# A two-block transformer kernel: ada pieces placed among x's turns, ScalarE writes that scale and shift, padded rotary queries, square sums in two passes

## The chip, the core and the metric

The kernel runs on one core of a Trainium2 chip. Five engines work from queues of their own and meet at semaphores: TensorE (PE, its weight loads listed apart as PEld), VectorE (DVE), ScalarE (ACT), GpSimd (POOL) and SyncE (SP), which here only issues DMAs. The metric is the time of one execution in microseconds. "Time" below is the device time of a run; "span" is the stretch that the profiler shows of one execution.

## What is computed

Two layers' worth of blocks on 512 tokens of width 2048, with 256 context tokens in the first. All is float32.

```python
# first block (cut)
sh_x, sc_x, gt_x = split(silu(c) @ w_ada + b_ada, 3)         # the same for the context with c_ctx
h_x = rms_norm(x, norm_g) * (1 + sc_x) + sh_x
h_c = rms_norm(ctx, norm_g) * (1 + sc_c) + sh_c
px, pc = split_cols(h_x @ w_in), split_cols(h_c @ w_in)
oa, ob, oc, od = mixer_a(px[0:4], ...), mixer_b(...), mixer_c(...), mixer_d(...)   # four attentions
x = x + gt_x * (concat([oa, ob, oc, od]) @ w_out)
# mixer d: q and k have 128 plain and 64 rotary columns per head;
#   s = q_nope @ k_nope.T + q_rope @ k_rope.T, softmax, @ v, times silu(gate)
# second block: an even and an odd layer
h = rms_norm(x, g) @ w_in;  q = rms_norm(heads(h_q), q_gain);  k = rms_norm(heads(h_k), k_gain)
#   heads are 64 wide, so each 128-row tile holds two heads; pooling, top-k attention, window attention
x = x + (silu(gate) * o) @ w_out
```

## The kernel before

**Data and products.** Activations lie transposed: a tile is 128 features by the tokens. A product with large weights is made of three TensorE passes over numbers of the type fp32r: each operand is split into `hi` (the fp32 value rounded on a write by ScalarE) and `lo` (what is left), and `w_hi*h_hi`, `w_hi*h_lo`, `w_lo*h_hi` are summed in PSUM. Weights come as groups of 1 MB (`raw`, two buffers). ScalarE's `hi(G, half)` rounds half a group (L862), GpSimd's `lo(G, half)` subtracts (L1180), and each waits for TensorE to leave that half's buffer. A group of the late part is 16 tiles of features by three passes of 128x512, which is 48 matmuls.

**The opening** (`start` on each engine). SP loads six tiles of x and context, then the pieces of w_ada (`ada`, four pieces of 1 MB to a chunk, eight chunks, a ring of four buffers) and the weight blocks. ScalarE sums squares and takes the root of each tile (L783, L786), VectorE scales (L1314), TensorE turns the tile in 16 transposes into the four PSUM banks of `acc`, and `x_out` empties them into `X6`: banks 0 and 1 by VectorE, 2 and 3 by ScalarE. Then TensorE takes the four pieces of chunk 0 (`piece`), ScalarE copies the row (`ada_row`, L797), TensorE folds it (`fold`), VectorE adds the bias (`columns`, L1328 and L1333). Each chunk gives four tiles' scale (chunks 0 to 3) or shift (chunks 4 to 7). A small table of distances (L1299, L1301) is made first of all.

**Eight blocks** follow: for the gates of mixers a and b, products run as soon as four tiles' scale is there, without the shift. `scaled(c)` on VectorE multiplies (L1343), ScalarE rounds (L803), VectorE subtracts (L1352). TensorE works through block n in two halves; after each of the four column tiles j of half 0 it takes a piece of chunk n+1, and after j = 1 of half 1 the fold. From block 5 on the full h is made for later groups: GpSimd adds `hi` and `lo` back together once the block that read them is done (`full_sum`, L1164), VectorE scales and shifts the context tile (L1359), adds the shift to the latent tile (L1361), ScalarE rounds 768 columns (L809), VectorE subtracts (L1369). After the last block VectorE empties the banks (`gates_out`, L1379); the first group of mixer a's keys waits for all of it (`raw_out` 8) and then, tile by tile, for `h_full`.

**Mixer d.** Its last ten groups, of kinds kn and vn, multiply plain fp32 data with no split (`acc<-raw,ckv_t`). VectorE's `norm` takes a reciprocal (L1417) and two scalings (L1427, L1436). In `attend`, `scores(n)` makes for each of 16 units a 512 and a 256 wide product with 128 rows (`k_latent`), and into the same place one with 64 rows (`k_rope,q_rope`): rows 0 to 63 or 64 to 127 of the tile by the head's parity.

**The late part** (`late`) is a list of groups written out in `plan`. Of kind norm and kvn there are 27. For them ScalarE squares the product (`post`, L1108), TensorE sums the squares of 64 rows with one fp32 matmul by a matrix of ones (`first`, for the group before, after tile k = 3 of the next group; k = 5 after a group of kind wout), ScalarE takes the root and VectorE the reciprocal and the scaling (`after`, L1782, L1797). `hooks` put attention work between the tiles of the groups of kind silu: units dsa(0), dsa(1) after tiles k = 3 and 7 of the first, units swa(0), swa(1) after k = 7 and 15.

## Time and profile before

| | us |
|---|---|
| median of 3 runs | 2930.26 |
| lowest and highest | 2928.46 and 2931.2 |
| the profiled execution | 2931.68 |
| its span | 2929.8 |
| TensorE busy | 2823.2 (96%) |
| VectorE / ScalarE / GpSimd busy | 1116.1 / 959.2 / 1077.7 |

The profiled execution takes 1.88 us more than its span; a change of the span is taken as a change of the time. A row of the timeline has the start in us, the duration, the engine, the line, the operation, output and inputs, the count, and in brackets the idle time before it with what ended it. Matmuls overlap, so their pace is read from the distance of the starts.

### The profile page before, as it was taken

The numbers are of one execution on the slowest core, as the hardware profiler recorded it, in microseconds if no ns is written. First come the engines' busy times: TensorE is split into PE (matmuls) and PEld (weight loads), VectorE is DVE, ScalarE is ACT, GpSimd is POOL, SyncE is SP. The second block draws the span as 40 slices with busy tenths as digits, with TensorE's granted clock in tenths as the row PEclk, the third lists the DMA queues.
The fourth block names the chain that finished last, engine by engine and source line by source line (L and its number), as shares of the span: only waits on it lengthen the run. The fifth ranks groups of instructions, "written<-read, shape, count | busy, mean of one in ns | idle before, by whom it ended". The sixth has DMA issues, their size and how long they took to land.

```text
span 2929.8 us, 34587 instructions
## 1 busy us (share of the span) xinstructions
PE 2823.2 (96%) x14062; PEld 2176.6 (74%) x14062; DVE 1116.1 (38%) x1848; ACT 959.2 (33%) x1479; POOL 1077.7 (37%) x529
## 2 busy tenths in 40 slices
PE   5979999989999998899999999999999999999999
PEld 3557788878778874478887677766787877777787
DVE  4164323142322143322212468744223455566411
ACT  4222332242233221332222312365322223666411
POOL 1253213213321330135543343444455343545443
PEclk9989999999999999999999999999999999999999
DMA  8844412213575231413433233322443333322442
GB/s 324 298 154 124 136 58 72 72 26 101 172 180 115 62 83 43 129 36 112 122 90 87 72 101 87 101 71 74 148 122 104 100 87 94 87 76 78 138 123 83
DMA packets 456605, 318.28 MB, mean 109 GB/s; under 512 B 32352, under 2 KB 404960, under 8 KB 455680
## 3 DMA queue, kind: packets, MB, share of 16 engines
q1 hardware_dynamic: 424400, 280.09, 32.9%
q10 hardware_dynamic: 32048, 35.98, 4.8%
q8 instruction: 112, 1.84, 0.3%
q14 instruction: 45, 0.37, 0.0%
HBM read 299.14 MB, written 28.95 MB: 112 GB/s over the span
## 4 chain that ended last, share of the span: by engine, by line
PE 92%; DVE 3%; DMA 2%; ACT 1%; issue 1%; POOL 1%; SPq 0%; ACTq 0%; DVEq 0%; POOLq 0%
PE acc L1863 77%; PE aux L1863 8%; PE ssq L1866 3%; PE ssq L1863 3%; DMA raw<-in_w_in 1%; PE aux L1866 1%; POOL w_lo L1180 1%; DVE rstd L1417 1%; DVE x_t L1361 0%; PE acc L1866 0%; DVE x_t L1359 0%; DMA dist_mask_sb<-in_dist_mask 0%; DVE h_lo L1369 0%; ACT w_hi L862 0%; DVE p L1489 0%
## 5 line engine op out<-in xcount | busy, mean ns | idle before, releaser
L1180 POOL TENSOR_TENSOR w_lo<-raw,w_hi 128x1024 fp32r<-128x1024 f32 x362 | 868.7, 2400 | 1698.8 <-ACT w_hi L862 1698.6
L1863 PE MATMUL acc<-h_hi,w_hi 128*128 128x512 f32 (+1 forms) x3232 | 1214.0, 393 | 33.6 <-DVE gate_raw L1379 19.7
L1863 PE MATMUL acc<-h_hi,w_lo 128*128 128x512 f32 (+1 forms) x3232 | 1172.2, 380 | 0.0
L1863 PE MATMUL acc<-h_lo,w_hi 128*128 128x512 f32 (+1 forms) x2464 | 872.7, 376 | 0.0
L862 ACT ACTIVATE w_hi<-raw 128x1024 fp32r<-128x1024 f32 x362 | 383.0, 1059 | 1171.0 <-PE acc L1863 1077.0
L1863 PEld LDWEIGHTS acc<-h_hi,w_hi 128*128 128x128 f32 x3232 | 585.0, 188 | 206.9 <-issue 77.2
L1863 PEld LDWEIGHTS acc<-h_hi,w_lo 128*128 128x128 f32 x3232 | 583.6, 188 | 119.4
L1863 PEld LDWEIGHTS acc<-h_lo,w_hi 128*128 128x128 f32 x2464 | 440.9, 189 | 91.1 <-issue 10.6
L1863 PE MATMUL acc<-out_t_lo,w_hi 128*128 128x512 f32 x768 | 299.0, 389 | 0.0
L1417 DVE RECIPROCAL rstd<-rstd 128x512 f32<-128x512 f32 (+1 forms) x29 | 118.0, 4070 | 352.8 <-ACT rstd L906 352.7
L1863 PEld LDWEIGHTS acc<-out_t_lo,w_hi 128*128 128x128 f32 x768 | 144.3, 188 | 29.0
L1863 PE MATMUL acc<-k_t,q_t 64*128 64x256 f32 (+6 forms) x592 | 130.3, 434 | 2.8 <-DVE v_nat L1407 1.3
L1782 DVE RECIPROCAL rstd<-rstd 128x512 f32<-128x512 f32 x27 | 90.5, 3352 | 73.5 <-ACT rstd L1083 73.5
L1866 PE MATMUL ssq<-ident_sb,p 128*128 128x128 f32 x744 | 107.7, 281 | 6.3 <-ACT p L960 5.3
L1866 PEld LDWEIGHTS ssq<-ident_sb,p 128*128 128x128 f32 x744 | 82.3, 142 | 33.3 <-issue 23.3
L1863 PEld LDWEIGHTS acc<-k_t,q_t 64*128 64x128 f32 (+1 forms) x592 | 67.4, 194 | 39.0 <-issue 33.9
L995 ACT ACTIVATE p_t<-ssq 128x768 f32<-128x768 f32 (+2 forms) x64 | 49.3, 771 | 110.0 <-PE ssq L1866 110.0
L1736 DVE TENSOR_TENSOR scaled<-acc,rstd_n 128x512 f32<-128x512 f32 x62 | 42.9, 692 | 108.7 <-PE acc L1863 108.6
L1679 DVE COPY p<-cols_sb 128x4 f32<-128x4 f32 x32 | 66.2, 2068 | 0.0
L1069 ACT ACTIVATE p<-p,u_neg_max 128x257 f32<-128x257 f32 (+1 forms) x128 | 60.3, 473 | 9.8 <-DVE u_neg_max L1686 9.6
L1797 DVE SCALAR_TENSOR_TENSOR q_t<-scaled,cols_sb,rstd 128x512 f32<-128x512 f32 x24 | 62.8, 2617 | 0.9
L1754 DVE SCALAR_TENSOR_TENSOR h_lo<-x_t,cols_sb,h_hi 128x512 fp32r<-128x512 f32 x32 | 41.4, 1294 | 54.0 <-DMA x_t_dram<-x_t 54.0
(235 smaller groups left out, 2337.2 us busy)
## 6 DMA issues: line engine op xcount, KB each, us to landing
raw<-in_w_in SPq DMA_DIRECT2D x52, 1024.0 KB, 5.9
raw<-in_even_w_in SPq DMA_DIRECT2D x41, 1024.0 KB, 5.6
raw<-in_odd_w_in SPq DMA_DIRECT2D x36, 1024.0 KB, 5.6
ada_ring<-in_w_ada SPq DMA_DIRECT2D x32, 1024.0 KB, 5.5
gate_ring<-in_w_ada SPq DMA_DIRECT2D x16, 1024.0 KB, 7.0
raw<-in_w_out SPq DMA_DIRECT2D x16, 1024.0 KB, 5.9
raw<-in_even_w_out SPq DMA_DIRECT2D x16, 1024.0 KB, 5.9
raw<-in_odd_w_out SPq DMA_DIRECT2D x16, 1024.0 KB, 6.5
```

Source lines behind the costliest of these rows:

```text
L862: A.activation(WH[half][:], RAW[G.rs][:, half * HALF * P:(half + 1) * HALF * P], ACT.Copy).then_inc(S["hi_done"], 1)
L995: A.activation(PTS[u % 2][:, 0:nk], SSQ[:, 0:nk], ACT.Copy).then_inc(S["pt_ready"], 1)
L1069: e = A.activation(p, p, ACT.Exp, bias=LNG[:, c:c + 1], scale=-1.0, accum_out=LSM[:, c:c + 1])
L1180: G_.tensor_tensor(WL[half][:], RAW[G.rs][:, half * HALF * P:(half + 1) * HALF * P], WH[half][:].bitcast(F32), ALU.subtract).then_inc(S["l ...
L1417: Vv.reciprocal(RS, RS).then_inc(S["rs_done"], 1)
L1679: Vv.tensor_copy(p[:, :, :, 256], sink.unsqueeze(2).to_broadcast([P, 2, 2]))
L1736: e = Vv.tensor_tensor(Y[G.y][:], a, RSN[:], ALU.mult)
L1754: Vv.scalar_tensor_tensor(out=ktile(H2L, G.j, SEQ), in0=ktile(X, G.j, SEQ), scalar=norm_gain(G), in1=ktile(H2H, G.j, SEQ).bitcast(F32), op ...
L1782: Vv.reciprocal(RS[:], RS[:]).then_inc(S["rs_made"], 1)
L1797: e = Vv.scalar_tensor_tensor(out=out_of(G), in0=y[:], scalar=gain(G), in1=RS[:], op0=ALU.mult, op1=ALU.mult)
L1863: return M.matmul(out_, lhsT, rhs, start=start, stop=stop, skip_group_check=True)
L1866: return M.transpose(out_, in_, IDENT[rows, rows])
```

## The change

- **Order of loads.** SP loads all six tiles, then ada pieces 0 and 1, the first weight block, pieces 2 and 3, and only then the distance table's inputs. Its products on TensorE come after fold 0, its sums on VectorE after `scaled(0)`.
- **Turns.** TensorE turns tiles 0 to 3, piece 0, tile 4, pieces 1 and 2, tile 5, piece 3. ScalarE empties a turned tile two steps later than it squares (`x_out(t - 2)`), and of odd tiles only bank 3; VectorE takes the other three.
- **Scale and shift.** `scaled_hi`, `full_hi` apply scale or shift as they round; VectorE's one `scalar_tensor_tensor` (L1381, L1399 of the changed kernel) gives `lo`. VectorE, not GpSimd, adds `hi` and `lo` back. The context is made apart, one chunk to each of blocks 4 to 7 (`context`). `full_hi` stands ahead of the next weights' `hi`, and ScalarE empties the last banks.
- **Padded queries.** GpSimd clears 128x2048 numbers (`QRP`, on h1_lo's last tiles), VectorE copies each head's 64 rows into them, and `scores` multiplies 128 rows.
- **Square sums.** ScalarE writes the square twice, as fp32 and rounded; GpSimd subtracts; TensorE sums `hi` and `lo` in two fp32r passes. Between two groups of which the first is a norm and the second is not silu, the sum comes after k = 10, and ScalarE's and VectorE's `after` behind `hi(G.next, 0)` and `take(G)`; elsewhere after k = 6 (norm or wout before) or 3.

```diff
@@ SP start @@
-                for t in range(2):
+                for t in range(6):
                     sp.dma_start(ktile(XNAT, t, D), x_rows(t)).then_inc(S[f"xi{t}"], 16)
...
-                ada(0)
+                ada(0, (0, 1))
                 weights(blocks[0])
+                ada(0, (2, 3))
@@ ScalarE start @@
-                    if t:
-                        x_out(t - 1)
+                    if t >= 2:
+                        x_out(t - 2)
+                blocks = item["blocks"]
+                x_out(4)
+                hi(blocks[0], 0)
                 x_out(5)
...
+                    act.wait_ge(S["scales"], c + 1)
                     for k in range(4 * c, 4 * c + 4):
-                        act.wait_ge(S["hs_ready"], k + 1)
-                        A.activation(lat(H1H, k), lat(X6, k), ACT.Copy).then_inc(S["hs_hi"], 1)
+                        A.activation(lat(H1H, k), lat(X6, k), ACT.Identity,
+                                     scale=ADA[:, 2 * (KT + k):2 * (KT + k) + 1]).then_inc(S["hs_hi"], 1)
...
+                def context(c):
+                    act.wait_ge(S["ada_cols"], 5 + c)
+                    for k in range(4 * c, 4 * c + 4):
+                        A.activation(ctxt(X6, k), ctxt(X6, k), ACT.Identity, bias=ADA[:, 2 * k + 1:2 * k + 2],
+                                     scale=ADA[:, 2 * (KT + k) + 1:2 * (KT + k) + 2]).then_inc(S["hc_ready"], 1)
+                    act.wait_ge(S["hc_ready"], 4 * c + 4)
+                    for k in range(4 * c, 4 * c + 4):
+                        e = A.activation(ctxt(H1H, k), ctxt(X6, k), ACT.Copy)
+                    e.then_inc(S["hc_hi"], 1)
@@ VectorE start @@
                 def full(c):
+                    dve.wait_ge(S["half_done"], 2 * item["blocks"][4 + c].g + 2)
                     for k in range(4 * c, 4 * c + 4):
+                        Vv.tensor_tensor(lat(X6, k), lat(H1L, k).bitcast(F32), lat(H1H, k).bitcast(F32),
+                                         ALU.add).then_inc(S["h_sum"], 1)
@@ VectorE, mixer d @@
+                for h in range(4):
+                    rows = slice(64 * (h % 2), 64 * (h % 2) + 64)
+                    Vv.tensor_copy(ktile(QRP, h, SEQ)[rows, :], ktile(QR, h // 2, SEQ)[rows, :])\
+                      .then_inc(S["pad_done"], 1)
...
+                if G.kind == "kn" and G.j == 1:
+                    pad_queries()
@@ TensorE, scores @@
-                            e = mm(dst, ktile(QR, h // 2, SEQ)[rows, qt * P:(qt + 1) * P],
-                                   ktile(KR, h // 2, TOK)[rows, key:key + w], False, True)
+                            e = mm(dst, QRP[:, h * SEQ + qt * P:h * SEQ + (qt + 1) * P],
+                                   ktile(KR, h // 2, TOK)[:, key:key + w], False, True)
@@ late: ScalarE, GpSimd, TensorE @@
-                        A.activation(scratch(G)[0][:], Y[G.y][:], ACT.Square).then_inc(S["sq_made"], 1)
+                        A.activation(scratch(G)[0][:], Y[G.y][:], ACT.Square)
+                        A.activation(squares(G)[0][:], Y[G.y][:], ACT.Square).then_inc(S["sq_made"], 1)
...
+                        pool.wait_ge(S["sq_made"], G.norm + 1)
+                        need(pool, "sq_summed", G.norm)
+                        G_.tensor_tensor(low[:], scratch(G)[0][:], high[:].bitcast(F32), ALU.subtract)\
+                          .then_inc(S["sq_low"], 1)
...
-                        mm(SSQ[:, 0:SEQ], ONES64[:], scratch(G)[0][:], True, True).then_inc(S["sq_summed"], 1)
+                        mm(SSQ[:, 0:SEQ], ONESR[:], high[:], True, False)
+                        mm(SSQ[:, 0:SEQ], ONESR[:], low[:], False, True).then_inc(S["sq_summed"], 1)
...
-                    at_first = 5 if prev is not None and prev.kind == "wout" else 3
+                    at_first = 10 if behind(G, prev) else 3
+                    if prev is not None and prev.kind in ("wout", "norm") and not behind(G, prev):
+                        at_first = 6
```

TensorE's queue at the start of the program, up to the first block's first product, before. `ada_ring` holds the pieces, `rel_bias_sb` belongs to the distance table:

```order
L1863 MATMUL ssq<-onehot_sb,rel_bias_sb 32x512
L1863 MATMUL ssq<-onehot_sb,rel_bias_sb 32x128
L1866 MATMUL acc<-ident_sb,x_natural 128x128 x96
L1863 MATMUL aux<-ada_ring,cond_silu 32x512 x16
L1863 MATMUL ssq<-fold_sb,ada_rows 128x2 x4
L1863 MATMUL acc<-h_hi,w_hi_60 128x512
```

And now:

```order
L1917 MATMUL acc<-ident_sb,x_natural 128x128 x64
L1914 MATMUL aux<-ada_ring,cond_silu 32x512 x4
L1917 MATMUL acc<-ident_sb,x_natural 128x128 x16
L1914 MATMUL aux<-ada_ring,cond_silu 32x512 x8
L1917 MATMUL acc<-ident_sb,x_natural 128x128 x16
L1914 MATMUL aux<-ada_ring,cond_silu 32x512 x4
L1914 MATMUL ssq<-fold_sb,ada_rows 128x2 x4
L1914 MATMUL ssq<-onehot_sb,rel_bias_sb 32x512
L1914 MATMUL ssq<-onehot_sb,rel_bias_sb 32x128
L1914 MATMUL acc<-h_hi,w_hi_60 128x512
```

The table's two products moved behind the fold, and three of the four pieces moved among the turns of tiles 4 and 5.

ScalarE's queue from block 6's `hi(G.next, 0)` to the first rows of mixer a's groups, before (`w_hi` is `hi`, `ada_rows` is `ada_row`, `h_hi` is `full_hi`):

```order
L862 ACTIVATE w_hi_60<-raw_59 128x1024
L797 ACTIVATE ada_rows<-aux 128x512
L862 ACTIVATE w_hi_61<-raw_59 128x1024
L809 ACTIVATE h_hi<-x_t_116 128x768 x4
L862 ACTIVATE w_hi_60<-raw_58 128x1024
L862 ACTIVATE w_hi_61<-raw_58 128x1024
L809 ACTIVATE h_hi<-x_t_116 128x768 x8
```

The same stretch of block 6 now:

```order
L898 ACTIVATE w_hi_60<-raw_59 128x1024
L833 ACTIVATE x_t_117<-x_t_117,ada_sb 128x256 x4
L837 ACTIVATE h_hi<-x_t_117 128x256 x4
L811 ACTIVATE ada_rows<-aux 128x512
L898 ACTIVATE w_hi_61<-raw_59 128x1024
L826 ACTIVATE h_hi<-x_t_117,ada_sb 128x512 x4
L898 ACTIVATE w_hi_60<-raw_58 128x1024
```

Eight small writes for the context now stand between the weights' `hi` and the row that the fold waits for, and the rounding of h stands ahead of the next weights.

GpSimd's queue in two neighbouring late groups of kind norm, before and then now:

```order
L1180 TENSOR_TENSOR w_lo_62<-raw_59,w_hi_60 128x1024
L1180 TENSOR_TENSOR w_lo_63<-raw_59,w_hi_61 128x1024
L1180 TENSOR_TENSOR w_lo_62<-raw_58,w_hi_60 128x1024
L1180 TENSOR_TENSOR w_lo_63<-raw_58,w_hi_61 128x1024
L1180 TENSOR_TENSOR w_lo_62<-raw_59,w_hi_60 128x1024
```

```order
L1210 TENSOR_TENSOR w_lo_62<-raw_59,w_hi_60 128x1024
L1210 TENSOR_TENSOR w_lo_63<-raw_59,w_hi_61 128x1024
L1304 TENSOR_TENSOR squares_lo<-squares_173,squares_hi 128x512
L1210 TENSOR_TENSOR w_lo_62<-raw_58,w_hi_60 128x1024
L1210 TENSOR_TENSOR w_lo_63<-raw_58,w_hi_61 128x1024
L1304 TENSOR_TENSOR squares_lo<-squares_173,squares_hi 128x512
```

Each norm group gained one subtraction behind both halves of the next weights.

## Rows read from the trace of the kernel before

**Rows 1.** Timeline, all engines, 0 to 60 us: the opening's end.
```profile
39.11 3.64 PE L1863 MATMUL aux<-ada_ring,cond_silu 128*32 128x512 f32 x32
...
42.82 0.60 ACT L797 ACTIVATE ada_rows<-aux 128x512 f32<-128x512 f32 x1 [2.95 <-PE aux L1863]
...
43.47 1.05 PE L1863 MATMUL ssq<-fold_sb,ada_rows 128*128 128x2 f32 x8 [0.72 <-ACT ada_rows L797]
...
51.89 0.76 PE L1863 MATMUL acc<-h_hi,w_hi 128*128 128x512 f32 x1 [7.37 <-DVE h_lo L1352]
```
**Rows 2.** Stretches: PE, PEld, DVE, ACT, POOL busy; clock, DMA share, GB/s.
```profile
32.00:34.00 2.00, 0.04 (x1) 0.07 (x2) 2.00 (x3) 2.00 (x3) 0.00 (x0) 1.00 0.76 278
...
50.00:52.00 2.00, 0.11 (x1) 0.14 (x1) 1.94 (x4) 1.18 (x3) 0.00 (x0) 0.50 1.06 389
```
**Rows 3.** What PE's matmuls waited for, whole span: total us, times, longest.
```profile
PE acc L1863 <- DVE gate_raw L1379: 19.7, 1, 19.7
PE aux L1863 <- DVE k_rope L1436: 17.4, 2, 9.3
...
PE acc L1863 <- DVE h_lo L1352: 9.1, 4, 7.4
...
PE ssq L1863 <- POOL sq_sum L1274: 2.6, 2, 1.3
```
**Rows 4.** Timelines of ScalarE and TensorE in block 5.
```profile
150.59 0.60 ACT L797 ACTIVATE ada_rows<-aux 128x512 f32<-128x512 f32 x1
...
153.35 0.95 PE L1863 MATMUL ssq<-fold_sb,ada_rows 128*128 128x2 f32 x8
```
**Rows 5.** Timelines between block 7 and the first keys, and behind.
```profile
190.83 2.02 DVE L1369 TENSOR_TENSOR h_lo<-x_t,h_hi 128x768 fp32r<-128x768 f32 x1
...
201.99 2.48 DVE L1379 COPY gate_raw<-acc 128x512 f32<-128x512 f32 x4
...
204.52 1.01 PE L1863 MATMUL acc<-h_hi,w_hi 128*128 128x512 f32 x2 [19.67 <-DVE gate_raw L1379]
...
209.70 0.51 PE L1863 MATMUL acc<-h_hi,w_lo 128*128 128x512 f32 x2
210.05 0.51 PE L1863 MATMUL acc<-h_hi,w_hi 128*128 128x512 f32 x2
```
**Rows 6.** Timeline of VectorE, mixer d's second kn group.
```profile
1138.11 4.95 DVE L1417 RECIPROCAL rstd<-rstd 128x768 f32<-128x768 f32 x1 [1.03 <-ACT rstd L906]
```
**Rows 7.** Timelines of TensorE: fp32 products of one shape; a unit of attention d.
```profile
1185.73 8.34 PE L1863 MATMUL acc<-raw,ckv_t 128*128 128x512 f32 x19
...
1245.71 1.02 PE L1863 MATMUL acc<-k_latent,q_t 128*128 128x512 f32 x2
...
1248.97 0.33 PE L1866 MATMUL aux<-ident_sb,o_nat 128*128 128x128 f32 x1
```
**Rows 8.** Timelines of ScalarE and GpSimd around the last late norm group.
```profile
2471.84 1.06 ACT L862 ACTIVATE w_hi<-raw 128x1024 fp32r<-128x1024 f32 x1 [2.14 <-PE acc L1863]
2477.28 1.06 ACT L862 ACTIVATE w_hi<-raw 128x1024 fp32r<-128x1024 f32 x1 [4.38 <-PE acc L1863]
2478.25 0.61 ACT L1108 ACTIVATE squares<-scaled 128x512 f32<-128x512 f32 x1
...
2483.63 1.06 ACT L862 ACTIVATE w_hi<-raw 128x1024 fp32r<-128x1024 f32 x1 [2.14 <-PE acc L1863]
...
2478.42 2.37 POOL L1180 TENSOR_TENSOR w_lo<-raw,w_hi 128x1024 fp32r<-128x1024 f32 x1 [3.04 <-ACT w_hi L862]
...
2494.22 1.04 POOL L1249 TENSOR_TENSOR p<-p,u_inv 128x512 f32<-128x512 f32 x1
```
**Rows 9.** Timelines behind the last norms: TensorE at dsa(1), swa(1); VectorE before swa(1).
```profile
1897.10 0.47 PE L1863 MATMUL acc<-select_mask,ident_r 128*128 128x256 f32 x2 [2.02 <-DVE q_t L1797]
...
2489.99 1.13 PE L1863 MATMUL acc<-k_t,q_t 64*128 64x256 f32 x8
...
2489.22 0.08 DVE L1686 DVE_READ_ACCUMULATOR2_ANT u_neg_max<- 128x1 f32 x1
```

217 lines of the change are left out of this document (126 added, 91 removed).

## The prediction

> **What bounds the kernel now.** TensorE is busy for 2823.2 of 2929.8 us, so a change is worth what it takes from TensorE's idle time or from the passes it makes. I read the waits of its matmuls first [rows 3]. The largest single wait is 19.7 us, for VectorE's emptying of the banks after the eighth block; then come two waits of 17.4 together in mixer d, for VectorE's scaling, and four of 9.1 for `lo` of h, of which one is 7.4. The change touches the first and the third, and it may lengthen the second. Next I read the opening: the first block's first product starts at 51.89, after 7.37 us of nothing [rows 1]. The loads are no reason for that: the DMA engines run dry within the stretch 32 to 34 (share 0.76, then nothing is asked for until ring buffers come free), so all tiles, chunk 0 and the first weights lie there by about 33.5 [rows 2]. Last I read the pace of passes: a half group of 24 late matmuls takes 2477.28 - 2471.84 = 5.44 us, 0.227 each, and the half with a square sum 2483.63 - 2477.28 = 6.35, so one sum costs 0.91 [rows 8].
>
> **The opening.** Before, all four pieces stood behind the last turn: 3.64 from 39.11, then the row copy (0.60), the fold (1.05), and multiply, round, subtract [rows 1]. Now three of four pieces are placed among the turns, and ScalarE no longer waits for a turn before the next square. The loads then set the pace: a piece is 1.05 MB, 2.7 us at 389 GB/s [rows 2], so if piece 3 is there at 33.5, piece 2 was at 30.8. It takes 0.9 (a quarter of 3.64), the last turn about 2, and ends near 33.8; piece 3 goes to 34.8; row copy and fold take 0.65 and 1.05, to 36.6; two small additions 0.5. The distance table's products come there too, but beside ScalarE's writes. Two writes of 0.6 by ScalarE and one subtraction of about 0.8 lead to 39.3. One step can slip, so I take 40.4: **11.5 us less**, between 8 (a turn and its copies late by 3) and 13 (no slip).
> Before, the clock stood at 0.50, which is 1.2 GHz, when the first block began, after 7.37 idle, while at 32 to 34, with TensorE idle as well but for a shorter time, it was 1.00, which is 2.4 GHz [rows 1, 2]. The new order leaves no gap like the 7.37, so I let the first products run at full clock. A start at half clock cost the first keys 2.4 us (below); here, with shorter passes of pieces among them, I take 1.9, between 0 and 2.4.
>
> **The blocks.** VectorE's multiply goes, so the wait at the start of blocks 1 to 3 goes too: 9.1 - 7.4 = 1.7 less [rows 3]. Against it, on ScalarE eight context writes stand ahead of `ada_row` in blocks 4 to 6. Their price isn't in the trace; 1024 columns take 1.06 and 512 take 0.60 [rows 1, 8], so 256 cost at most 0.37 and in a row about 0.27; with one wait for themselves eight are 2.6 (2.2 to 3.0). The row's copy ended at 151.19 and the fold began at 153.35 [rows 4], a slack of 2.1. So each fold comes 0.5 late, queued behind it on TensorE the rest of the block: three times 0.5, **1.5 more** (0 to 3). The sum of the blocks is 1.7 + 1.9 - 1.5 = **2.1 less**.
>
> **Behind the last block.** The 19.67 us [rows 5] were VectorE making h for the tiles with everything behind `full_sum`, and only then four copies of 2.48 together. Now three copies by ScalarE run inside the block and the fourth, 0.60, right behind it: with semaphores 0.85. That is **18.8 less**. What is late next? Weights: `hi(G.next, 1)` then takes 1.06 and GpSimd's `lo` 2.4, to 4.4 us after the block's end, and TensorE wants them after eight tiles of three pairs at 0.35 [rows 5], 8.4 us after it starts. h: the last four tiles need four sums, four writes and four subtractions. VectorE's h_lo took 2.02 while GpSimd ran [rows 5]; even so they end about 9.5 us after the block, and tile 12 is wanted after 0.85 + 12.6. Both are covered. The clock: the first keys ran their first eight pairs in 209.70 - 204.52 = 5.18 us and not in 8 x 0.35 [rows 5]: **2.4 less**.
>
> **Mixer d.** One call of `scores` takes 1248.97 - 1245.71 = 3.26 us [rows 7]. Products of one shape take 0.43 each, a load of weights with each of them (19 in 8.34) [rows 7]. By that pace 4 of 512 and 4 of 256 columns are 1.71 + 0.85 = 2.56. The 0.70 more lies where 128 rows and 64 rows alternate. Padding makes all of them one shape with the same columns. Two ends: nothing (rows 64 of the k tile still cost) and 0.70; I take 0.65, as the fp32 products with fresh weights each time are the same case: 16 x 0.65 = **10.4 less**.
> The Trainium skill, "TensorE: Matmul & The Clock Gate", Part 2, "Step-by-step: what each phase is for", says that weight loads are pulled ahead of running matmuls where row groups don't conflict or the background buffer takes them, and that row count doesn't matter for the time; by it the padding is free and the gain the full 0.70. The same page's table in "Why this matters for your kernels" speaks against padding: products with few rows could run side by side in separate row groups. No run here shows that, and beside a 128-row product there is no free group.
> The padding costs VectorE four copies of 64x512. Nearest are the four copies of 128x512 that took 2.48 out of PSUM [rows 5]; out of SBUF they can be up to half as long: 1.3 to 2.5. They stand ahead of the reciprocal at 1138.11, which had waited 1.03 [rows 6], and TensorE waits 9.3 for what follows it [rows 3]: 0.3 to 1.5 more; I take **0.7 more**. GpSimd's clearing is hidden in its idle time.
>
> **Late sums.** Two fp32r passes are 2 x 0.227 = 0.45 in place of 0.91 [rows 8]: 0.42 to 0.46 less. 27 x 0.42 = **11.3 less**. GpSimd's low square must be there: counted from a group's end, ScalarE rounds weights (1.2) and squares twice (to 2.4), GpSimd subtracts weights (to 3.6) and then the low square, for which the nearest row has 1.04 and I allow 1.3 [rows 8], to 4.9. TensorE asks for it after 11 tiles, 11 x 0.68 = 7.5: slack 2.6. On the two places where silu follows it asks after 7 tiles, 4.8, so 0.1 late; and there everything behind is late by the new place: 3 tiles are 2.05. dsa(1) had already waited 2.02 for the scaled queries [rows 9], so it waits **2.1 more**; for swa(1) VectorE was done at 2489.30 and TensorE came at 2489.99 [rows 9], so of 2.4 late **1.7** show. After the two closing wout groups the sum is asked for one tile, 0.68, later, and the two waits of 2.6 [rows 3] shrink by **1.3**. Together 11.3 - 2.1 - 1.7 + 1.3 = **8.8 less**.
>
> The Trainium skill, "SBUF — State Buffer", "Who interferes with whom", speaks against the new work on GpSimd: GpSimd and VectorE operations with two SBUF inputs hold one port pair alone, and the other blocks. The row of 2.02 [rows 5] agrees. VectorE's longest work in a norm group is not waited for by TensorE, so the sum is as above by either.
>
> **Sum.** 11.5 + 2.1 + 18.8 + 2.4 + 10.4 - 0.7 + 8.8 = 53.3. Against the profiled execution's 2931.68 that is 2878.4; the median is 1.4 lower, so I say **2877**. With each term at its ends it is 2868 to 2888.
>
> **The rivals.**
> *Part of the new order waits elsewhere* (0.16). SP's queue holds every load in one line, and ScalarE has the block's longest list; if chunk 2's pieces, which stand behind the distance table, or `full_hi` come late, TensorE waits in blocks. For it: ScalarE's eight new writes. Against it: the DMA engines move 389 GB/s when asked [rows 2], which is a block's 5.2 MB in 13.5 us, and a block has 48 passes of 0.227, four pieces of 0.9 and a fold, 15.5 at least. Price: 1.5 to 3 us in each of six blocks, so 2886 to 2895.
> *The row change isn't what costs 0.70* (0.07): an accumulating pair on one bank would cost the same with 128 rows. Against it: the 19 products accumulate too. Price 10.4: 2887.
> *More than forecast* (0.12): the opening starts at 38.5, the dsa and swa delays are taken up by later hooks, folds aren't late: 2877 - 2 - 3.8 - 1.5, so 2866 to 2871.
> *Slower than before* (0.02): GpSimd's low square misses its place in each norm group. Each group then waits for it, and the wait comes 25 times. It decides from 2.6 us of delay; the whole gain of 53 is gone when each is 2.1 beyond that, 4.7 later than I work out, which would need two more weight subtractions ahead of it. Price: 2877 + 25 x 2.5, so 2940.
> That the change doesn't do what it says: the blocks' order would still give the 18.8; it is inside the first rival.
>
> **Chances.** Forecast 0.62, and 0.01 for anything near no change. The range 2865 to 2894 holds all but the slow case and the far part of the first rival. A measurement here tells about 0.2%, 6 us, from no change: faster 0.97, same 0.01, slower 0.02.
>
> **What would show it.** First block product near 40, clock 1.00; folds in blocks 4 to 6 with ScalarE's row as releaser, 0.5 each; the 19.67 replaced by under 1 us; `scores` in 2.6; the half group with a sum in 5.9; a wait of 4 at dsa(1). Wrong would be a wait of more than 1 us in blocks 1 to 3, VectorE's or ScalarE's h as releaser in the first keys, or the low square as TensorE's releaser in norm groups.

## The result, and the profile after

The changed kernel takes **2883.11 us** (median of 4 runs, 2882.11 to 2885.66) where the kernel before, in the same session, took 2930.02 (4 runs, 2928.46 to 2931.2): a ratio of 0.9838, 95% interval 0.9826 to 0.985. The prediction said 2877 and a range of 2865 to 2894: faster was right, the time is 6.1 us above the point and inside the range. The profiled execution has a span of 2880.3 against 2929.8, 49.5 us less, where the terms summed to 53.3. Of the 6.1 us, 3.7 are the terms' (the profiled execution took 2882.11, forecast 2878.4); the rest is that the profiled execution of before lay 1.4 above the median that the forecast used, and the one of the changed kernel lies 1.0 below its own.

The waits of TensorE's matmuls come first, as in [rows 3] (what waited and for what: total us, times, longest):

```profile
PE aux L1914 <- DVE k_rope L1472: 18.1, 2, 10.0
...
PE ssq L1914 <- ACT ada_rows L811: 3.9, 4, 1.1
PE aux L1914 <- DMA ada_ring<-in_w_ada: 3.1, 1, 3.1
PE acc L1914 <- ACT gate_raw L859: 2.2, 1, 2.2
```

The 19.7 for the gate's banks has become 2.2, and the four for `lo` of h (9.1) are down to one of 1.4. New are 3.1 for a load of an ada piece, and three of the four waits in the line of `ada_rows`, near 1.1 each.

A total of waits doesn't say where time went, because a wait is not all that a late engine costs. So I took the same instruction in both traces and subtracted its starts; what the difference grows by between two places is what the stretch between them gained.

| the same instruction | before | after | earlier by | the stretch gained | forecast |
|---|---|---|---|---|---|
| first block product | 51.89 | 40.57 | 11.3 | 11.3 | 11.5 |
| last fold, in the seventh block | 170.14 | 163.73 | 6.4 | -4.9 | +2.1 |
| first keys | 204.52 | 180.76 | 23.8 | 17.4 | 18.8 |
| first square sum behind them | 227.01 | 201.01 | 26.0 | 2.2 | 2.4 |
| first scores of mixer d | 1194.99 | 1167.31 | 27.7 | 1.7 | -0.7 |
| total sum of the first residual stream | 1472.11 | 1432.60 | 39.5 | 11.8 | 10.4 |
| last transposes | 2925.65 | 2876.13 | 49.5 | 10.0 | 8.8 |

One row is badly wrong: the blocks were to gain 2.1 us and lost 4.9. The other six are within 2.4 of the forecast, three above it and three below.

**The blocks.** TensorE, then ScalarE, in the fifth block (n = 4) of the changed kernel:

```profile
124.34 1.05 PE L1914 MATMUL ssq<-fold_sb,ada_rows 128*128 128x2 f32 x8 [1.05 <-ACT ada_rows L811]
```
```profile
119.41 1.06 ACT L898 ACTIVATE w_hi<-raw 128x1024 fp32r<-128x1024 f32 x1 [8.07 <-PE acc L1914]
120.37 2.07 ACT L833 ACTIVATE x_t<-x_t,ada_sb 128x256 f32<-128x256 f32 x4
122.47 1.34 ACT L837 ACTIVATE h_hi<-x_t 128x256 fp32r<-128x256 f32 x4
123.71 0.58 ACT L811 ACTIVATE ada_rows<-aux 128x512 f32<-128x512 f32 x1
```

The eight context writes take from 120.37 to 123.8, 3.4 us where I had 2.6. The four with scale and shift, which also read and write the same buffer, are half a microsecond each (2.07 for four), the four plain ones a third (1.34). The row's copy behind them ends at 124.3, and the fold waits 1.05. The same happens at 144.04 (1.08) and 163.73 (1.05). That makes 3.2 us. The rest is in the stretches of TensorE behind the wait (columns as in [rows 2]; the clock is the third figure from the right, ahead of the DMA share and GB/s):

```profile
124.00:126.00 2.00, 1.66 (x11) 1.57 (x12) 1.44 (x5) 0.29 (x1) 0.00 (x0) 0.96 1.05 386
126.00:128.00 2.00, 2.00 (x6) 1.54 (x6) 0.00 (x0) 0.00 (x0) 0.00 (x0) 0.50 0.98 357
128.00:130.00 2.00, 2.00 (x8) 1.59 (x7) 0.05 (x1) 0.06 (x1) 0.00 (x0) 0.69 0.00 0
```

The clock stands at 0.50, which is 1.2 GHz, from 126 to about 129, and a stretch of 2 us holds 6 instructions and not 10 or 14. From 130 on it is 1.00 (2.4 GHz) again. The same drop is there behind the second late fold (0.58 and 0.57 at 146 to 150) and not behind the third. From one late fold to the next it is 19.70 us with a drop between them; in the run turn5 below, where the first drop is missing, the same stretch is 18.07, so a drop costs 1.6 us.

**The opening.** TensorE's rows, to be read against [rows 1]:

```profile
26.19 1.07 PE L1914 MATMUL aux<-ada_ring,cond_silu 128*32 128x512 f32 x8
30.40 1.94 PE L1914 MATMUL aux<-ada_ring,cond_silu 128*32 128x512 f32 x8 [3.14 <-DMA ada_ring<-in_w_ada]
32.26 2.63 PE L1917 MATMUL acc<-ident_sb,x_natural 128*128 128x128 f32 x16
...
36.60 1.05 PE L1914 MATMUL ssq<-fold_sb,ada_rows 128*128 128x2 f32 x8 [0.72 <-ACT ada_rows L811]
...
40.57 0.76 PE L1914 MATMUL acc<-h_hi,w_hi 128*128 128x512 f32 x1 [1.40 <-DVE h_lo L1381]
```

The product is at 40.57 (forecast 40.4), but the fold begins at 36.60, where the forecast had its end. Piece 2 waits 3.14 for its load and runs at 30.40 (forecast 30.8), and behind that gap the clock is 0.56 to 0.58: piece and turn take 1.94 and 2.63 in place of 1.07 and 1.97. From 34 to 40 the clock is at 1.00 again, while TensorE is busy for 2.3 of the last 4 us, and it is low a second time when the blocks begin:

```profile
36.00:38.00 2.00, 1.14 (x9) 1.05 (x10) 0.27 (x2) 0.55 (x1) 0.00 (x0) 1.00 1.06 390
38.00:40.00 2.00, 1.18 (x4) 0.26 (x4) 1.05 (x3) 1.82 (x3) 0.00 (x0) 1.00 1.05 387
40.00:42.00 2.00, 1.43 (x4) 1.17 (x5) 2.00 (x4) 1.69 (x3) 0.24 (x1) 0.62 1.05 386
42.00:44.00 2.00, 2.00 (x8) 0.85 (x10) 0.94 (x2) 0.00 (x0) 2.00 (x1) 0.52 1.05 386
```

**Behind the last block.** TensorE, then ScalarE, to be read against [rows 5]:

```profile
180.76 0.62 PE L1914 MATMUL acc<-h_hi,w_hi 128*128 128x512 f32 x2 [2.25 <-ACT gate_raw L859]
```
```profile
175.33 2.06 ACT L833 ACTIVATE x_t<-x_t,ada_sb 128x256 f32<-128x256 f32 x4
177.43 1.34 ACT L837 ACTIVATE h_hi<-x_t 128x256 fp32r<-128x256 f32 x4
178.67 2.04 ACT L859 ACTIVATE gate_raw<-acc 128x512 f32<-128x512 f32 x4
```

All four copies run behind the block, because the last eight context writes stand ahead of them; the block ended at 178.5.

**Mixer d and the late sums** are shown with their experiment and their steps below.

### The profile page after: what moved, and what is told of

It reads as the page before. It is cut to its first block, busy times and chain, and to the rows that moved or that the text cites. A ratio compares the mean times of both kernels' runs of the same rounds, so it can differ in the third digit from the quotient of the medians.

```text
span 2880.3 us, 34712 instructions
## 1 busy us (share of the span) xinstructions
PE 2795.4 (97%) x14062; PEld 2178.5 (76%) x14062; DVE 1062.8 (37%) x1836; ACT 984.7 (34%) x1539; POOL 1093.5 (38%) x541
## 3 DMA queue, kind: packets, MB, share of 16 engines
q8 instruction: 113, 1.85, 0.3%
## 4 chain that ended last, share of the span: by engine, by line
PE 92%; DMA 2%; DVE 2%; ACT 2%; issue 1%; POOL 1%; SPq 1%; ACTq 0%; DVEq 0%; POOLq 0%
PE acc L1914 77%; PE aux L1914 7%; PE ssq L1917 3%; PE ssq L1914 3%; DMA raw<-in_w_in 2%; PE aux L1917 1%; POOL w_lo L1210 1%; DVE rstd L1453 1%; DMA ada_ring<-in_w_ada 0%; ACT w_hi L898 0%; SPq L673 0%; ACT x_t L833 0%; DVE p L1535 0%; ACT p_t L1031 0%; DMA nbr_bias<-nbr_bias_dram 0%
## 5 line engine op out<-in xcount | busy, mean ns | idle before, releaser
L1914 PEld LDWEIGHTS aux<-p_t,v_nat 128*64 128x64 f32 x768 | 40.8, 136 | 26.4 <-issue 26.4
```

Of the source, the lines that this page charges most:

```text
L1914: return M.matmul(out_, lhsT, rhs, start=start, stop=stop, skip_group_check=True)
```

## The experiments

From session to session the kernel before gave 2927.77 to 2934.62 us, so a single run's time says little by itself; single runs are read by the places in their traces that the edit touches.

**1. What made the blocks longer.** The first run removes the late row by order alone; the second leaves it late and fills TensorE's time with products whose results nobody reads.

```diff
@@ rows_first: ScalarE start, in the loop over blocks @@
-                    if n >= 4:
-                        context(n - 4)
                     if n < 7:
                         ada_row(n + 1)
+                    if n >= 4:
+                        context(n - 4)
@@ fill_wait: TensorE, fold, ahead of the wait for ada_row @@
+                    if chunk >= 5:
+                        for i in range(5):
+                            mm(AUX[:, 512 * ((chunk + 1) % 2):512 * ((chunk + 1) % 2) + 512], WH[1][:, 0:P],
+                               lat(H1H, 4 * ((chunk - 1) % 4)), True, True)
```

> The changed kernel with one move on ScalarE: in blocks 4 to 6 the copy of the ada row stands ahead of the eight context writes, not behind them. Theory: the copy then ends near 121.1 and the fold, asked for at 123.3, finds it there. The three waits of 1.05 to 1.08 for the row go (3.2 us), and the clock, which stood at 0.50 to 0.58 for about 3.5 us behind two of those waits, stays at 1.00 (3.4 us): first keys at 174.1 in place of 180.76, the whole at about 2876.5. Rival: the clock fell there for another reason (the passes themselves): only the waits go, first keys at 177.5, about 2880. Second rival: the context tiles come late to the first keys, where TensorE then waits over 1 us.

Measured: 2876.32 us (4 runs, 2875.23 to 2879.28), ratio to before 0.9817, interval 0.9801 to 0.9834. First keys at 173.72, 7.0 us earlier than in the changed kernel (forecast 6.7): 1.2 us at each of the three folds and 1.7 at each of two stretches behind them. The folds have no wait, and the context tiles were not late. The stretch at half clock is gone:

```profile
126.00:128.00 2.00, 2.00 (x10) 1.64 (x9) 0.86 (x2) 0.87 (x1) 0.00 (x0) 1.00 0.96 346
```

> The changed kernel with five throwaway products of 512 columns (5 x 0.227 = 1.1 us) ahead of each of the three folds that wait for ScalarE's row, their results in a bank that is overwritten later. ScalarE's order stays. Theory: it is TensorE's own idle 1.1 us that lowers the clock behind the folds; filled, the clock stays at 1.00 in 124 to 131 and 144 to 151, and the first keys start 3.4 us earlier, at 177.3, although the folds are no earlier. Rival: the clock fell for another reason; first keys at 180.8 and the same stretches at 0.50 to 0.69.

Measured: 2880.9 us (one run, span 2879.1). Here the folds are as late as before, since five passes take the time of the wait, and yet:

```profile
126.00:128.00 2.00, 2.00 (x11) 1.70 (x11) 0.33 (x2) 0.00 (x0) 0.00 (x0) 1.00 1.04 384
```

Between 47.1 and 148.5 it gained 3.2 us on the changed kernel, 1.6 at each of the two places (the first keys came at 178.46 and not at 177.3, as its opening was 0.9 us slower). So the theory stands against its rival: it was TensorE's own idle time that lowered the clock, and of the 7.0 us that the late row cost, 3.2 were its echo in the clock and 3.8 the waits with the slower start behind them.

This one run is borne out by all traces together. Eight of them have the late row: the changed kernel and the runs d_grouped, loads, turn5, loads2, copies_first, low_first and pads_late. Of their 24 waits of 1.04 to 1.08 us, 14 were followed by 3.4 us at 0.50. Of the 15 folds without a wait at these places (the kernel before, rows_first, fill_wait, best and best2), none was. Which wait has the echo changes from run to run: the first in six of the eight, the second in seven, the third in one. The code of these blocks is the same in all eight, so whether a given wait lowers the clock differs from execution to execution; what decides it stays open.

**2. Behind the last block.** The last context tiles go behind the gate's copies and the next weights.

```diff
@@ copies_first: ScalarE start @@
-                    if n >= 4:
+                    if 4 <= n < 7:
                         context(n - 4)
...
                     hi(G.next, 1)
+                context(3)
                 full_hi(3)
```

> The changed kernel with the last context tiles on ScalarE behind the four copies of the gate's banks and the rounding of the next weights, not ahead of them. Theory: the context writes held the copies; now three of them run inside the last block and the fourth right behind it, and TensorE waits 0.85 us for the first keys in place of 2.25, 1.4 less. [...] Rival: the context tiles 12 to 15 come late to the first keys (wanted 12.6 us behind their start), and TensorE waits for them over 1 us.

Measured: 2878.84 us (one run). ScalarE and TensorE:

```profile
175.63 1.10 ACT L859 ACTIVATE gate_raw<-acc 128x512 f32<-128x512 f32 x2
...
178.85 0.60 ACT L859 ACTIVATE gate_raw<-acc 128x512 f32<-128x512 f32 x1 [0.76 <-PE acc L1915]
```
```profile
179.50 0.62 PE L1915 MATMUL acc<-h_hi,w_hi 128*128 128x512 f32 x2 [0.69 <-ACT gate_raw L859]
```

The wait is 0.69 and the gain at this place 1.5 us, and no tile is late. This is the picture that the prediction had drawn (0.85). The rest of the 4.3 us by which this one run is shorter came further on, in places that the edit doesn't touch, and isn't credited to it.

**3. The opening.** Three orders, all with the last turn ahead of piece 2; two of them move loads.

```diff
@@ turn5, loads, loads2: TensorE start @@
                 piece(0, 1)
-                piece(0, 2)
                 x_turn(5)
+                piece(0, 2)
                 piece(0, 3)
@@ loads: SP start @@
-                ada(0, (0, 1))
+                ada(0)
                 weights(blocks[0])
-                ada(0, (2, 3))
@@ loads: ScalarE start @@
                 x_out(4)
-                hi(blocks[0], 0)
                 x_out(5)
...
                 ada_row(0)
+                hi(blocks[0], 0)
                 scaled_hi(0)
@@ loads2: as loads, but weights(blocks[0]) behind the three small loads, and in scaled_hi @@
                     for k in range(4 * c, 4 * c + 4):
+                        if k == 2:
+                            hi(blocks[0], 0)
```

> The changed kernel with another opening: the four pieces of chunk 0 are loaded ahead of the first weights, the last turn stands ahead of pieces 2 and 3, and ScalarE rounds the first weights behind the row copy. Theory: the order of the loads sets the opening (piece 2 waited 3.14 us for its load, which stood behind 1.05 MB of weights, and the last turn stood behind the piece): piece 3 is done near 31.5, the row near 32.1, the first block product near 36.7 in place of 40.57, bound by the first weights' rounding, 3.9 us less; with the clock at 1.00 for the first products another 1.5 less. The whole at 2877.5 to 2879. Rival: the small steps between ScalarE and VectorE set it, and the first product comes at 39 or later.

Measured: 2881.18 us (4 runs, 2877.63 to 2884.62), ratio 0.983, interval 0.9816 to 0.9845, which is not distinguished from the changed kernel's. The first half of the theory held, the second didn't: the row's copy ran at 31.56, but the product came at 39.56 and not at 36.7:

```profile
31.56 0.60 ACT L809 ACTIVATE ada_rows<-aux 128x512 f32<-128x512 f32 x1 [1.98 <-PE aux L1913]
...
34.72 1.06 ACT L897 ACTIVATE w_hi<-raw 128x1024 fp32r<-128x1024 f32 x1 [2.56 <-DMA raw<-in_w_in]
35.68 2.54 ACT L817 ACTIVATE h_hi<-x_t,ada_sb 128x512 fp32r<-128x512 f32 x4
35.86 2.35 POOL L1209 TENSOR_TENSOR w_lo<-raw,w_hi 128x1024 fp32r<-128x1024 f32 x1 [34.56 <-ACT w_hi L897]
...
36.50 5.69 DVE L1380 SCALAR_TENSOR_TENSOR h_lo<-x_t,ada_sb,h_hi 128x512 fp32r<-128x512 f32 x3 [2.83 <-ACT h_hi L817]
```

The weights now land last, ScalarE waits for them ahead of h, and VectorE's subtractions fall beside GpSimd's. The clock was forecast at 1.00 for the first products and wasn't: it was 1.00 up to 36, as there was no long gap ahead of the pieces, and 0.50 from 36 to 42, behind a stretch in which TensorE did next to nothing (0.10 of the 2 us from 34 to 36).

> The changed kernel with TensorE's last turn of x ahead of piece 2 and not behind it; loads and ScalarE as in the changed kernel. Theory: piece 2 still waits for its load until 30.4, but the turn (ready at 26.4) is behind it no more, so piece 3 runs when its own load lands, near 33.1 in place of 34.82, and the first block product starts at 38.9 in place of 40.57, 1.7 less. TensorE's longest idle time in there falls from 3.1 to about 1.3 us, so the clock (0.56 to 0.58 between 30 and 34) should stay at 1.00 there. Rival: piece 3's load lands no earlier than 34.8 and nothing is gained.

Measured: 2886.14 us (one run); the first product at 42.44, 1.9 later than in the changed kernel. The rival held. Piece 3's load was not there before 35.01, so the earlier turn only opened a longer gap, at the end of which the piece ran at half clock, 1.94 us, and the fold too, 1.87:

```profile
30.43 1.07 PE L1914 MATMUL aux<-ada_ring,cond_silu 128*32 128x512 f32 x8 [1.27 <-DMA ada_ring<-in_w_ada]
35.01 1.94 PE L1914 MATMUL aux<-ada_ring,cond_silu 128*32 128x512 f32 x8 [3.51 <-DMA ada_ring<-in_w_ada]
```

The turn between pieces 2 and 3, which I had taken for an obstacle, costs next to nothing where it stands, and it keeps TensorE at work: in fill_wait, which has the changed kernel's opening, piece 3 still waited 0.76 behind the turn and ran at 34.55.

> The opening of the run before last (all four pieces loaded ahead of the first weights, last turn ahead of pieces 2 and 3) with two repairs: the three small loads of the distance table stand ahead of the first weights, and ScalarE rounds these weights behind the first two writes of h and not ahead of all. In that run the row was there at 31.56 as forecast, but the table's products waited 2.64 for their loads, and VectorE's three subtractions of 5.69 us together ran beside GpSimd's subtraction of weights. Theory: the first two tiles of h are done before GpSimd starts, near 36, and the first product starts when the first weights are subtracted, near 38.5 in place of 39.56. Rival: VectorE's subtractions are slow for another reason than GpSimd, then the product stays at 39.5.

Measured: 2884.36 us (one run); the first product at 40.41, with a wait of 3.82 for GpSimd's low weights. In this run piece 3 could start 1.65 later than in the run loads (32.08 and 30.43); counted from there, the product came after 8.3 us and not 9.1. VectorE and GpSimd:

```profile
36.27 1.42 DVE L1381 SCALAR_TENSOR_TENSOR h_lo<-x_t,ada_sb,h_hi 128x512 fp32r<-128x512 f32 x2 [0.95 <-ACT h_hi L819]
38.36 5.11 DVE L1381 SCALAR_TENSOR_TENSOR h_lo<-x_t,ada_sb,h_hi 128x512 fp32r<-128x512 f32 x2 [0.68 <-ACT h_hi L819]
```
```profile
37.80 5.13 POOL L1210 TENSOR_TENSOR w_lo<-raw,w_hi 128x1024 fp32r<-128x1024 f32 x2 [36.51 <-ACT w_hi L898]
```

The same instruction takes 0.71 us alone and 2.56 beside GpSimd's subtraction, which itself takes 2.57 here and 2.35 to 2.41 elsewhere. The rival, another reason than GpSimd, is out. The gain stayed away since the rounding and subtraction of the weights, 3.7 us from 36.68 to the product, are now the longer chain. By the Trainium skill, "SBUF — State Buffer", "Who interferes with whom", VectorE and GpSimd share one pair of ports when VectorE reads two operands from SBUF. The trace agrees, and it adds the price: GpSimd's began first (37.80 against 38.36), and VectorE paid nearly all of it, 1.85 us against some 0.2.

So no order of these loads was better by more than the opening varies anyway: in nine runs with the changed kernel's opening the first product came between 40.30 and 41.91.

**4. Mixer d.** Half of the row changes, without padding.

```diff
@@ d_grouped: TensorE, scores @@
                         e = mm(dst, q, kk[:, kv * TOK + key:kv * TOK + key + w], True, m != "d")
-                        if m == "d":
-                            e = mm(dst, QRP[:, h * SEQ + qt * P:h * SEQ + (qt + 1) * P],
-                                   ktile(KR, h // 2, TOK)[:, key:key + w], False, True)
+                    if m == "d":
+                        rows = slice(64 * (h % 2), 64 * (h % 2) + 64)
+                        for c, key, w in parts:
+                            e = mm(ACC[:, u % 2, c:c + w], ktile(QR, h // 2, SEQ)[rows, qt * P:(qt + 1) * P],
+                                   ktile(KR, h // 2, TOK)[rows, key:key + w], False, True)
```

> The changed kernel with unpadded queries (64 rows) in mixer d's scores as before, but in another order: both products with 128 rows first, then both with 64 rows, so two changes of the row count in a unit in place of four. The padding copies are still made. Theory: the cost lies in the change, 0.19 us each (3.26 before, 2.58 with padding, the 0.68 over four changes): a unit's scores take 2.95, and mixer d is 16 x 0.37 = 5.9 us longer than with padding. Rival: every pass with 64 rows pays for its own weight load, whatever stands ahead: only the 128-row product that followed a 64-row one gets its 0.20 back, scores take 3.06, 8 us longer than with padding.

Measured: 2891.0 us (one run). The changed kernel's unit, against [rows 7]:

```profile
1205.89 1.02 PE L1914 MATMUL acc<-k_latent,q_t 128*128 128x512 f32 x2
1206.75 1.02 PE L1914 MATMUL acc<-k_rope,q_rope_padded 128*128 128x512 f32 x2
...
1208.47 0.27 PE L1917 MATMUL aux<-ident_sb,o_nat 128*128 128x128 f32 x1
```

and the grouped one, its matmuls and then its weight loads:

```profile
1201.77 1.46 PE L1914 MATMUL acc<-k_latent,q_t 128*128 128x512 f32 x4
1203.15 1.55 PE L1914 MATMUL acc<-k_rope,q_rope 64*128 64x512 f32 x4
```
```profile
1203.15 0.29 PEld L1914 LDWEIGHTS acc<-k_rope,q_rope 64*128 64x128 f32 x2 [0.33 <-issue]
1203.69 0.19 PEld L1914 LDWEIGHTS acc<-k_rope,q_rope 64*128 64x128 f32 x1 [0.24 <-issue]
```

A unit's scores take 3.26 us with four changes of the row count, 2.87 with two and 2.58 with none; the transpose behind them loses 0.06 after 64 rows. Per unit the grouped order is 0.35 us longer than padding, 5.6 us in mixer d (forecast 5.9, the rival said 8). The loads show how: the first 64-row load starts together with its product at 1203.15, the third, at 1203.69, and the fourth, at 1204.12, are done ahead of theirs. So a change costs, and 64 rows as such cost nothing. The rest of this run's 7.9 us above the changed kernel lies outside mixer d: the opening was 1.3 later, with more half clock behind it.

The Trainium skill, "TensorE: Matmul & The Clock Gate", Part 2, "Step-by-step: what each phase is for", has weight loads pulled ahead of running matmuls where row groups don't conflict or the load goes to the background buffer. The rows show a load that waits at the change and is pulled ahead between equals, and they give the price; whether a conflict of row groups is the reason, they don't show.

**5. The padding copies.**

```diff
@@ pads_late: VectorE step @@
-                if G.kind == "kn" and G.j == 1:
+                if G.kind == "kn" and G.j == 2:
                     pad_queries()
```

> The changed kernel with VectorE's four padding copies of mixer d (1.77 us in all) behind the rotation of the second keys, where VectorE is idle for 11.8 us, and not ahead of the second keys' reciprocal. Theory: that reciprocal started 0.71 us behind ScalarE's root because of the copies; without them TensorE's longer wait for the keys is 9.3 us in place of 10.0, and the stretch behind it, at half clock, is shorter: 0.7 to 1.4 us less between 1118 and 1127. Rival: the 0.69 us that the products behind the wait took more (6.43 in place of 5.74) have nothing to do with the wait's length; then 0.7 and no more.

Measured: 2882.22 us (one run). The wait for the keys is 9.3 in place of 10.0, and the place gained 0.6 us. The products behind it did not get faster, so the rival held: 0.7 and no more.

**6. The wait at dsa(1).** The sum ahead of a silu group is asked for two tiles earlier, with GpSimd's low square ahead of its second subtraction of weights.

```diff
@@ low_first: GpSimd late @@
+                    last = G.kind == "norm" and G.next.kind == "silu"
-                    if G.next is not None:
+                    if G.next is not None and not last:
                         lo(G.next, 1)
...
+                    if last:
+                        lo(G.next, 1)
@@ low_first: TensorE late @@
-                        at_first = 6
+                        at_first = 6 if prev.kind == "wout" else 4
```

> The changed kernel with GpSimd's low square ahead of its second subtraction of weights in the two groups that a silu group follows, and there the sum after 5 tiles and not after 7. Theory: the wait at dsa(1) of 4.74 grew by 2.7 because the sum stands 2.05 later, GpSimd's low square was 0.19 late and a group is 0.45 shorter; two tiles earlier give back 1.4 and the 0.19, so it is 3.2, and swa(1), which did not wait, still does not: 1.6 less in all. Rival: at swa(1) VectorE's write of q falls beside GpSimd's subtraction of weights again and takes 2.8 in place of 0.75 us, and TensorE waits up to 1 us there; a gain of under 1.

Measured: 2883.88 us (one run). The wait grew to 5.40. VectorE and ScalarE there (the sum's second pass began at 1849.61):

```profile
1849.53 2.44 DVE L1848 SCALAR_TENSOR_TENSOR q_t<-scaled,cols_sb,rstd 128x512 f32<-128x512 f32 x1
```
```profile
1852.06 0.69 ACT L1119 ACTIVATE rstd<-ssq,eps_sb 128x512 f32<-128x512 f32 x1 [4.36 <-DVE q_t L1848]
```

The theory fell. The sum was there at 1850.0, but the root goes into the one buffer that VectorE's write for the *group before* still reads, and that write, now beside GpSimd's moved subtraction, took 2.44 in place of the changed kernel's 1.41 (there it ran beside GpSimd's shorter low square, 1848.02 to 1849.33):

```profile
1848.47 1.41 DVE L1845 SCALAR_TENSOR_TENSOR q_t<-scaled,cols_sb,rstd 128x512 f32<-128x512 f32 x1
```

In the changed kernel that write ends at 1849.9 and the sum ends at 1850.3: two chains of nearly the same length, so an earlier sum alone can win 0.4 at most. The rival fell too: at swa(1) VectorE's write again took 0.75, and TensorE waited 0.23 there. I then moved that chain too, on top of the three moves that had helped:

```diff
@@ best2 over best: closing(G) is the last Q2 group @@
@@ VectorE late @@
-                    if not behind(G, prev):
+                    if not behind(G, prev) or closing(G):
                         after(prev)
...
-                    if behind(G, prev):
+                    if behind(G, prev) and not closing(G):
                         after(prev)
@@ TensorE late @@
-                        at_first = 6
+                        at_first = 5 if closing(prev) else 6
+                    if closing(G):
+                        at_first = 7
@@ GpSimd late: as in low_first, for closing(G) @@
```

> The changed kernel with three moves: ScalarE's row copy ahead of the context writes in blocks 4 to 6, its last context tiles behind the gate's copies, VectorE's padding copies behind the second keys' rotation. Theory: the places are independent, so the gains add: 7.0, 1.5 and 0.7 off 2883.1, which is 2874. Rival: the gap ahead of the first keys, 2.24 us, lowered the clock for the first keys in one of the kernels before and not in others; with 0.7 it stays at 1.00 and about 1 us more goes, 2873. Second rival: the gains meet a wait further on (the neighbour bias of mixer b comes by DMA and GpSimd, and the wait for it grew from 4.8 to 7.0 us with the earlier start), and less than 8 is left: 2876 or more.

> The kernel of the three moves with a fourth, at the end of the Q2 group: in the group ahead of dsa(0) TensorE sums after 8 tiles and not 11, VectorE normalises the group before ahead of scaling this one, GpSimd makes the low square ahead of its second subtraction of weights, and the next sum comes after 6 tiles and not 7. In the run that only asked for the last sum two tiles earlier the wait at dsa(1) grew to 5.40, since ScalarE's root waited until 1851.97 for VectorE's write of q (2.44 us beside GpSimd's subtraction), which still read the one buffer of the root. Theory: that chain (root, reciprocal 3.34, write 1.41) of the group before is the limit; started 2 us earlier it is out of the way, and the wait at dsa(1) falls from 4.74 to about 3.6: 1.2 us less than without the fourth move. Rival: VectorE's scaling comes later by the same amount and the wait stays at 4.7 or above.

Measured: `best`, that is rows_first, copies_first and pads_late together, 2874.48 us (5 runs, 2872.59 to 2877.45), ratio 0.9812, interval 0.9799 to 0.9826; it was forecast at 2874. `best2` 2872.96 (4 runs, 2871.63 to 2874.13), ratio 0.9805, interval 0.9791 to 0.9818, not distinguished from `best`. In the trace the wait at dsa(1) is 4.1 and not 3.6, and yet, from mixer d's scores to the products of dsa(1), `best2` gained 0.2 us on the changed kernel and `best` 0.3. The products behind the shorter wait ran at a lower clock (0.50 from 1845.2 to 1850; in `best` 0.82 from 1845 to 1848 and 0.71 from 1848 to 1852) and took back what the wait gave. Both are faster than either kernel of the case.

## Why the prediction was right, and where it was wrong

**What held.** The reading of the profile was right: the opening's order and the banks' emptying were the two large costs, and they gave 11.3 and 17.4 of 49.5 us. The row changes of mixer d were the third, and d_grouped settles that the change of row count is the cost. The slow case (GpSimd's low square missing its place) did not come near: TensorE waited 0.2 us for it in the whole span. Of the signs that the prediction had named, `scores` came out at 2.58 (2.6) and the wait at dsa(1) at 4.7 (4); the folds waited 1.05 and not 0.5, the first keys 2.25 and not under 1, and the clock at the first product was 0.50 and not 1.00. So the time lies inside the range partly by luck: one term was off by 7.0 us, and three others, one of them by chance, gave back 5.0.

**The opening, 11.5 forecast, 11.3 measured,** right in sum, with the allowance for a slip used up. Piece 2 came when forecast (30.40 for 30.8), so its gap was in the sum, though I hadn't spelled it out; it lies in the order of SP's queue, where `weights(blocks[0])` stands between pieces 1 and 2. What the sum lacked was the clock behind that gap, 0.9 on the piece and 0.7 on the turn. It made the fold a microsecond late, and the 1.1 kept for "one step can slip" paid for it.

"The new order leaves no gap like the 7.37, so I let the first products run at full clock" is the step that failed. The premise was true and the conclusion wrong: the 1.9 us for the clock were not there, and the first six products took 2.83 (40.57 to 43.40) as before. The gap of 3.14 is not the reason, for behind it the clock had come back to 1.00 for more than six microseconds, and the runs loads and fill_wait, in which it stayed at 1.00 from 28 to 34, had it at half for the first products too. In the nine traces with this opening TensorE was busy for 2.3 to 2.8 of the 4 us ahead of that product, and the clock fell in each; that those small waits are the cause wasn't tried. From 44.6 on the changed kernel is 0.4 better.

**The blocks, +2.1 forecast, -4.9 measured.** This is the wrong term, 7.0 us, more than the whole miss of the sum. The gain of 1.7 at the starts of blocks 1 to 3 came. Against it stand three things: the 1.9 of the clock; the price of the context writes, 3.4 and not 2.6, against a slack that I had at 2.1, so 3.8 us of waiting and slower starts and not 1.5; and what I didn't have at all, 3.2 us from half clock behind two of the three waits. The bound "0 to 3" was drawn for the wait alone. The first rival had the place ("ScalarE's eight new writes") and a price of 1.5 to 3 us a block; in each of two blocks it was 2.9 (wait and clock), in the third 1.2. In effect this rival came true in two blocks of its six at its own price and in a third below it, and the other terms covered it.

**Behind the last block, 18.8 forecast, 17.4 measured.** "Now three copies by ScalarE run inside the block" was wrong: the change as written had eight context writes ahead of them, the same queue item as in the blocks, and I had counted it there and not here. Moved behind, the wait is 0.69. The clock of the first keys gave 2.2 of 2.4.

**Between there and mixer d, -0.7 forecast, +1.7 measured.** The padding copies cost 0.7 of wait as forecast. The rest is what these 967 us do in any run. The wait for ScalarE's p in mixer b grew from 4.8 to 7.0, and one of 1.55 for GpSimd's low weights, at 248, is new. Against them the clock stood at half for 34 us in all and not for 44, although of the changes only the padding copies lie there. In the eleven traces of the experiments the same stretch took 964.6 to 969.0 us, with 31 to 48 us at half clock; the changed kernel has 966.3, the kernel before 968.0. I count the difference as chance.

**Mixer d, 10.4 forecast, 11.8 measured.** The unit fell by 0.68 in the scores and 0.06 in the transpose behind them: 0.74, where I had taken 0.65 by caution that no row asked for.

**Late sums, 8.8 forecast, 10.0 measured.** A group is 0.455 shorter (0.42 taken), so 27 give 12.3. dsa(1) waits 2.7 more (forecast 2.1), the two waits behind wout fell by 1.4 (1.3). Behind the longer wait at dsa(1) the clock is at half until 1859.8, which costs 1.7, but a second wait of 1.35 close behind it is gone. The last sum comes 0.35 late for GpSimd's low square. And swa(1) does not wait at all, where 1.7 was forecast. VectorE and GpSimd in the changed kernel:

```profile
2437.47 0.75 DVE L1845 SCALAR_TENSOR_TENSOR q_t<-scaled,cols_sb,rstd 128x512 f32<-128x512 f32 x1
```
```profile
2435.26 2.41 POOL L1210 TENSOR_TENSOR w_lo<-raw,w_hi 128x1024 fp32r<-128x1024 f32 x1 [2.72 <-ACT w_hi L898]
```

and the same two in the kernel before:

```profile
2484.91 2.79 DVE L1797 SCALAR_TENSOR_TENSOR q_t<-scaled,cols_sb,rstd 128x512 f32<-128x512 f32 x1
```
```profile
2484.77 2.39 POOL L1180 TENSOR_TENSOR w_lo<-raw,w_hi 128x1024 fp32r<-128x1024 f32 x1 [3.98 <-ACT w_hi L862]
```

Before, VectorE's write began 0.14 behind GpSimd's subtraction and took 2.79; after, it begins 0.20 ahead of that one's end and takes 0.75. The 2.04 us saved are the 2.05 by which the sum stands later. That this is the cause is argued from these rows and from the same prices in the opening (0.71 and 2.56). It wasn't tried by itself (in low_first the write took 0.75 again, but it began as GpSimd's ended), as the sum at its old place would have left GpSimd's subtraction unordered against a later write to the same memory. The place in the prediction is the step that took the write's duration from the trace of before as if it were the write's own.

**Open.** About 0.3 us of the late part is unaccounted for. What decides which waits lower the clock, no run tells: 14 of 24 of about 1.05 us did; of nine of 2.19 to 2.25 us ahead of the first keys, three did (rows_first, where the first keys lost 1.1 us by it, fill_wait and d_grouped), and the changed kernel's did not; at dsa(1) all twelve of 4.06 to 5.40 us had half clock around or behind them.

## What to carry to other kernels

When work is moved to another engine, write out that engine's queue at every place where the moved item appears, and ask at each of them what stands behind it: the eight context writes were costed in the blocks, but not at the last block, where the copies that TensorE waits for stood behind them. Price a new wait of TensorE at more than its length, because it can lower the clock for the passes behind; a wait that looks like 1 us was 2.9 in two of three places (14 of 24 over all traces had the echo), and putting one small copy first gave all of it back. And a VectorE duration with two operands in SBUF, read off a trace, holds only for what GpSimd did at that moment: look at GpSimd's row beside it before it goes into a sum.

## What the runs showed of the hardware

- A change between 128 and 64 rows from one fp32 product to the next costs 0.15 to 0.20 us; the weight load starts with the product there (both at 1203.15) and not ahead of it, and between products of 64 rows it is ahead, as between those of 128.
- TensorE idle for 1.04 to 1.08 us, with passes on both sides, was followed by 3.4 us at 1.2 GHz in 14 of 24 cases, and in none of three when the time was filled with throwaway products. Each such drop cost 1.6 us.
- In a row of four, ScalarE's writes of 128x256 take half a microsecond each with scale and shift from a column (2.07 for four) and a third without (1.34), where one plain copy of 128x512 is 0.6: half the columns take more than half the time.
- VectorE's subtraction of 128x512 with two operands in SBUF is 0.71 to 0.75 us alone and 2.4 to 2.8 beside a GpSimd subtraction of 128x1024 that began first, which stays near 2.4 to 2.6.
- GpSimd's subtraction of 128x512 takes 1.30 us, as the prediction allowed (1.3).
